# All down projections of the FFN stages in two rounds of 256 tokens, and the stages' activation tiles moved to 0 modulo 256 bytes

## The reference, cut to what matters

```python
def swiglu(u, w_gate_up, w_down):            # stage "f", D_FF = 2816
    gate, up = jnp.split(u @ w_gate_up, 2, axis=-1)
    return (jax.nn.silu(gate) * up) @ w_down

def sqrelu_mlp(x, w1, w2):                   # stages "m" and "n", D_FF_2 = 4096
    h = jax.nn.relu(x @ w1)
    return (h * h) @ w2
```

## Time and profile before

| | |
|---|---|
| median of 3 runs | 2082.5 us (2082.31 to 2082.69) |
| profiled execution, own time | 2082.63 us |
| its span | 2080.8 us |
| TensorE busy (matmul) | 2066.9 us, 99%, 12658 matmuls |
| VectorE, ScalarE, GpSimd busy | 1526.3, 982.3, 720.8 us |
| granted TensorE clock | full in all slices of the page |
| DMA | 188.44 MB, mean 91 GB/s |

### The profile page before, as it was taken

One profiled execution on the slowest core, in us unless ns is written; L12 is line 12 of the kernel. 1 busy time (PEld: TensorE's weight loads), 2 busy tenths in 40 slices (PEclk: granted clock), 3 DMA queues, 4 the chain that ended last, 5 costly groups with the idle time before them and its releaser, 6 DMA issues.

```text
span 2080.8 us, 32208 instructions
## 1 busy us (share of the span) xinstructions
PE 2066.9 (99%) x12658; PEld 1751.4 (84%) x12658; DVE 1526.3 (73%) x2087; ACT 982.3 (47%) x1656; POOL 720.8 (35%) x595
## 2 busy tenths in 40 slices
PE   9999999999999999999999999999999999999999
PEld 7888688888999998877789999988975678898988
DVE  6866775658988886388768787866578757877776
ACT  4433564445444444456554333344527755343433
POOL 2301520027443334064463232301147746333321
PEclk9999999999999999999999999999999999999999
DMA  6233135223333433211133323232530012333331
GB/s 182 91 107 86 52 102 172 71 66 95 102 103 102 121 93 101 81 51 52 41 92 104 120 82 122 83 120 89 152 80 1 2 52 75 118 93 110 93 110 51
DMA packets 293590, 188.44 MB, mean 91 GB/s; under 512 B 9280, under 2 KB 287040, under 8 KB 293440
## 3 DMA queue, kind: packets, MB, share of 16 engines
q1 hardware_dynamic: 293152, 186.18, 29.9%
q10 hardware_dynamic: 288, 0.21, 0.0%
HBM read 183.48 MB, written 2.10 MB: 89 GB/s over the span
## 4 chain that ended last, share of the span: by engine, by line
PE 94%; DVE 3%; ACT 1%; issue 1%; DMA 0%; POOL 0%; DVEq 0%; SPq 0%; ACTq 0%
PE ps L544 92%; PE ps L578 2%; DVE wl L517 1%; ACT wh L507 1%; DVE sb_small L3456 0%; DMA p_xt<-in_x 0%; DVE ns_x L3502 0%; DVE ns_x L3501 0%; DVE H L673 0%; DVE nt_pts L3484 0%; ACT XH L565 0%; ACT xb_x L565 0%; DVE tp_up L2296 0%; DVE tp_up L2309 0%; DVE XL L573 0%
## 5 line engine op out<-in xcount | busy, mean ns | idle before, releaser
L517 DVE TENSOR_TENSOR wl<-raw,wh 128x1024 fp32r<-128x1024 f32 (+1 forms) x334 | 429.4, 1300 | 231.9 <-ACT wh L507 231.3
L544 PE MATMUL ps<-xb_x,wh 128*128 128x256 f32 (+1 forms) x1584 | 388.8, 336 | 1.5 <-DVE st_k L2758 0.6
L507 ACT CAST wh<-raw 128x1024 fp32r<-128x1024 f32 (+1 forms) x334 | 322.0, 980 | 129.0 <-PE ps L544 119.4
L544 PEld LDWEIGHTS ps<-xb_x,wh 128*128 128x128 f32 x1584 | 267.2, 189 | 30.1 <-DVE H L673 0.9
L544 PE MATMUL ps<-tt_t,wh 128*128 128x256 f32 x1536 | 272.4, 279 | 0.9 <-ACT tp_q L2243 0.5
L544 PE MATMUL ps<-xb_x,wl 128*128 128x256 f32 (+1 forms) x792 | 265.0, 335 | 0.0
L544 PEld LDWEIGHTS ps<-tt_t,wh 128*128 128x128 f32 x1536 | 235.7, 188 | 4.8 <-ACT tp_q L2243 1.2
L544 PE MATMUL ps<-XH,wh 128*128 128x512 f32 (+1 forms) x616 | 227.2, 369 | 1.2 <-DVE H L703 0.8
L544 PE MATMUL ps<-XH,wl 128*128 128x512 f32 (+1 forms) x616 | 222.2, 361 | 0.0
L544 PE MATMUL ps<-XL,wh 128*128 128x512 f32 (+1 forms) x616 | 222.0, 360 | 0.0
L544 PE MATMUL ps<-tt_t,wl 128*128 128x256 f32 x768 | 213.1, 277 | 0.0
(11 more groups left out here) (448 smaller groups left out, 4566.9 us busy)
## 6 DMA issues: line engine op xcount, KB each, us to landing
raw<-in_mlp_w SPq DMA_DIRECT2D x128, 512.0 KB, 4.1
raw<-in_w_gate_up SPq DMA_DIRECT2D x44, 512.0 KB, 4.0
raw<-in_w_in SPq DMA_DIRECT2D x28, 512.0 KB, 3.7
raw<-in_sb_w_qkv SPq DMA_DIRECT2D x24, 512.0 KB, 3.6
raw<-in_w_down SPq DMA_DIRECT2D x22, 512.0 KB, 6.0
raw<-in_w_out_mix SPq DMA_DIRECT2D x16, 512.0 KB, 3.5
raw<-in_w_kv SPq DMA_DIRECT2D x16, 512.0 KB, 3.7
raw<-in_nsa_w_kv SPq DMA_DIRECT2D x12, 512.0 KB, 3.8
```

The source lines that it names most:

```text
L507: e.copy(shaped(WH[i % NH], i), source(i)).then_inc(*w_hi.up(i))
L517: e.tensor_tensor(shaped(WL[i % NH], i), source(i), shaped(WH[i % NH], i).bitcast(F), ALU.subtract).then_inc(*w_lo.up(i))
L544: return e.matmul(out, a, b, start=start, stop=stop, skip_group_check=True)
```

## The change

1. A new function `pe_down` replaces the call of `project` for downs. It runs over the tokens in two halves of 256 columns each, with all weight blocks in each half; the halves go to the two halves of the same PSUM bank. The matmuls double in number and halve in width. The release to VectorE stays one for the whole bank.
2. The plain activations of f and m move from xb (at PH0) to `XF` at PH0 - 64; those of n from XH and XL to `XN` at XAT + 192. The hidden tiles of f and m move from XAT to XAT + 192, those of n from PH0 to PH0 - 64. By the offsets in the code: XF and the hidden tiles of n start at 127232, XN and the hidden tiles of f and m at 77568; both are 0 modulo 256 (and 256 modulo 512). TT stays.
3. `sb_small` is placed ahead of rs, to make room for XN (which ends at 110336; rs then starts at 110400).

The last group of n keeps its own function, and reads the moved hidden tiles.

```diff
+    sb_small = sb("sb_small", [128, 64])
     RS0 = base[0]
...
-    sb_small = sb("sb_small", [128, 64])
     base[0] += 192
     PH0 = base[0]
     XB = Pair(*(Phase(PH0 + 4 * 8 * S * i, f"xb{i}").sb("x", [128, 8, S], R) for i in range(2)))
+    XF = Pair(*(Phase(PH0 - 64 + 4 * 8 * S * i, f"xf{i}").sb("x", [128, 8, S], R) for i in range(2)))
+    XN = Pair(*(Phase(XAT + 192 + 4 * 8 * S * i, f"xn{i}").sb("x", [128, 8, S], R) for i in range(2)))
...
-                act_hi(e, XB, "ff", o - 1, H[:, o - 1, :], col("ffn_norm", o - 1))
+                act_hi(e, XF, "ff", o - 1, H[:, o - 1, :], col("ffn_norm", o - 1))
...
                 if kind == "down":
                     t = take(e, key)
                     per = 8 // self.groups[g]
-                    project(e, self.units[n], self.hid[g % 2], f"{self.tag}{g}", t[:, :], key, nk=self.groups[g],
-                            c=128 * (c % per))
+                    self.pe_down(e, n, t, g, 128 * (c % per))
...
+        def pe_down(self, e, n, t, g, c):
+            i, hid = UI[self.units[n]], self.hid[g % 2]
+            e.wait_ge(*w_lo.at(i))
+            wh, wl = shaped(WH[i % NH], i), shaped(WL[i % NH], i)
+            last = self.groups[g] - 1
+            for half in range(2):
+                at = slice(256 * half, 256 * half + 256)
+                for k in range(last + 1):
+                    e.wait_ge(*x_lo.at(f"{self.tag}{g}", k))
+                    mm(e, t[:, at], wh[:, k, c:c + 128], hid.hi[:, k, at], k == 0, False)
+                    mm(e, t[:, at], wh[:, k, c:c + 128], hid.lo[:, k, at], False, False)
+                    f = mm(e, t[:, at], wl[:, k, c:c + 128], hid.hi[:, k, at], False, k == last)
+            f.then_inc(*proj.up(self.tag, n))
+            if not proj.final:
+                proj.name("unit", i)
...
-    ff = Ffn("f", GU, "ff", XB, XAT, "xa", [(v_made, ("xq", 7))])
-    fm = Ffn("m", [4] * 8, "m", XB, XAT, "st", [(g_made, ("fe", 7))])
-    fn = Ffn("n", [4] * 8, "n", X, PH0, "ns", [(v_made, ("nq", 7))], halves=True)
+    ff = Ffn("f", GU, "ff", XF, XAT + 192, "xa", [(v_made, ("xq", 7))])
+    fm = Ffn("m", [4] * 8, "m", XF, XAT + 192, "st", [(g_made, ("fe", 7))])
+    fn = Ffn("n", [4] * 8, "n", XN, PH0 - 64, "ns", [(v_made, ("nq", 7))], halves=True)
```

More of the change, by code:

```diff
@@ L1924, in act_xattn @@
         e.wait_ge(*h_new.at("xa", 7))
-        act_hi(e, XB, "ff", 7, H[:, 7, :], col("ffn_norm", 7))
+        act_hi(e, XF, "ff", 7, H[:, 7, :], col("ffn_norm", 7))
         act_square(e, "ff", 7, H[:, 7, :])
@@ L2005, in low @@
             e.wait_ge(*h_new.at("xa", o))
-            dve_lo(e, XB, "ff", o, H[:, o, :], col("ffn_norm", o))
+            dve_lo(e, XF, "ff", o, H[:, o, :], col("ffn_norm", o))
         for o in range(8):
@@ L2691, in act_stick @@
                 e.wait_ge(*h_new.at("st", o - 1))
-                act_hi(e, XB, "m", o - 1, H[:, o - 1, :], col("ng", 8 + o - 1))
+                act_hi(e, XF, "m", o - 1, H[:, o - 1, :], col("ng", 8 + o - 1))
                 act_square(e, "m", o - 1, H[:, o - 1, :])
@@ L2695, in act_stick @@
         e.wait_ge(*h_new.at("st", 7))
-        act_hi(e, XB, "m", 7, H[:, 7, :], col("ng", 15))
+        act_hi(e, XF, "m", 7, H[:, 7, :], col("ng", 15))
         act_square(e, "m", 7, H[:, 7, :])
@@ L2813, in low @@
             e.wait_ge(*h_new.at("st", o))
-            dve_lo(e, XB, "m", o, H[:, o, :], col("ng", 8 + o))
+            dve_lo(e, XF, "m", o, H[:, o, :], col("ng", 8 + o))
         for o in range(8):
@@ L3408, in act_nsa @@
                 e.wait_ge(*h_new.at("ns", o - 1))
-                act_hi(e, X, "n", o - 1, H[:, o - 1, :], col("ng", 24 + o - 1))
+                act_hi(e, XN, "n", o - 1, H[:, o - 1, :], col("ng", 24 + o - 1))
                 act_square(e, "n", o - 1, H[:, o - 1, :])
@@ L3412, in act_nsa @@
         e.wait_ge(*h_new.at("ns", 7))
-        act_hi(e, X, "n", 7, H[:, 7, :], col("ng", 31))
+        act_hi(e, XN, "n", 7, H[:, 7, :], col("ng", 31))
         act_square(e, "n", 7, H[:, 7, :])
@@ L3634, in low @@
             e.wait_ge(*h_new.at("ns", o))
-            dve_lo(e, X, "n", o, H[:, o, :], col("ng", 24 + o))
+            dve_lo(e, XN, "n", o, H[:, o, :], col("ng", 24 + o))
         for o in range(8):
```

## The result

| | before | after |
|---|---|---|
| median | 2082.7 us (2082.31 to 2082.98, 6 runs) | 2089.7 us (2087.67 to 2091.17, 6 runs) |
| ratio | | 1.0034 (1.0023 to 1.0045) |
| profiled execution, span | 2082.63, 2080.8 us | 2088.78, 2087.0 us |

The kernel is slower by 7 us, where 14 us less were forecast. The page of the kernel after, to set against the earlier trace rows: busy time by engine, the chain that ended last, and two groups of halved downs (count, busy us, mean ns).

A forecast was written before the change was run, and what follows sets the result against it. TensorE, busy 99%, was taken as the bound: matmul count times start-to-start distance. Pairs and downs -9.0 and -5.6, swallowed by waits +1.4, tail -1.3, nearer wait +0.5 gave -14.0: 2068.5 us from 2082.5; range 2064 to 2093.

The forecast's parts named there:

- the first rival: FFN stages: 256-column matmuls stay at 117.8 ns, 12.0 us more per stage; one slow stage 0.16, two or three 0.13.
- the quick cadence: FFN stages: aligned 256-column matmuls start 113.3 ns apart; holding in all three stages had chance 0.50, at 2068.5 us.
- Blocks of m: Stage m, one pair and four downs: 20.72 us becomes 20.40, 0.32 less in each of 14 blocks.
- Blocks of n: Stage n, one pair and four downs: 20.72 us becomes 20.40, 0.32 less in each of 14 blocks.
- Stage f: Gated stage, ten blocks of two pairs and four downs: 0.56 us less each, 5.6 in all, two blocks' gain swallowed.
- First jobs: Four plain 512-column jobs ahead of each stage's pairs, 288 matmuls: stay at 226.7 ns, taken as 0, at most 3.8 us less.
- the nearer x_lo wait: Last groups: half downs meet the fourth hidden tile's late low part; 0.2 us each in f and m, 0.1 in the tail.
- The tail: Its 192 half matmuls read the moved hidden tiles and go from 120.0 to 113.3 ns: 1.3 us less.
- The splitting: Downs in two halves: itself brings nothing, since 2 x 113.3 is 226.7 ns, what one whole down matmul takes.
- The rule of the Trainium skill: Matmul distance is N/2.4 + 2.5 ns, so splitting 1968 downs would add 4.9 us and the sum would be -9.
- The second rival: FFN tiles: 512-byte alignment is needed, so pairs stay at 120.0 ns and split downs cost 240.0; 2107 us, chance 0.08.

The follow-up runs named there:

- the rhythm held fast: Kernel after plus three extra same-remainder matmuls ahead of one pair each in n and m and f's first downs behind pairs, first jobs whole: 2074.4 us, ratio 0.9961.

## Why the prediction was wrong

**The step that failed** is the one by which the first rival was put at 0.29 in place of a half or more: "the quick cadence holds without a break, the stalls of the gated stage end in it". The rhythm does persist by itself; it does so in both forms. Behind the hiccups at four earlier downs f went on fast, behind the one at 627 us slow, and n was slow from its first pair. The forecast named what held it in check before (the plain products at 120.0) and that the change removes them, and then argued from rows in which they still stood. The earlier trace rows had shown that a wait can end either way; with nine waits in f, two of which left the slow rhythm, and nothing that resets, how f ended hung on the last of them. Why that one left the slow rhythm isn't shown; it did so again in the kernel with only the first jobs in halves. Of the stages the text said that their 512-column jobs "could put the first pair at 117.8 and nothing but a stall would take it out", which is what happened in n for the whole stage, and in f until its first stall at 510 us. In m the same jobs put the first pair at 113.3.

**Point by point.**

- Blocks of m: 20.40 us as forecast. The stage is 4.5 us shorter, for which 4.2 stood in the sum (14 x 0.32 less 0.3 for its first pairs).
- Blocks of n: 20.40 forecast, 21.20 measured; 6.3 us longer than before in place of 4.5 less. This is 10.8 of the 20 us between forecast and result.
- Stage f: from its first to its last combined product 1.7 longer in place of some 4.5 shorter, 6.2 of the 20 us; the last twelve downs behind it, slow as well, add 288 x 4.4 ns = 1.3.
- First jobs: taken at 0 with bounds from 0 to -3.8; measured +6.7 ns each, 288 x 6.7 = +1.9 us, and the three kernels with the weights moved show that it goes with the two remainders. I had bounded an operation that no row showed only from below ("From above, nothing"), and it came out above.
- Waits: the nearer x_lo wait is there before the last group of m (0.35 us for 0.2 forecast); in f it did not come. Not foreseen were the 0.1 us at the first down behind a pair in f. By themselves they cost nothing that counts; the one of them at 627 us cost the stage its rhythm.
- The tail, with its many waits, runs now in the one and now in the other rhythm; behind the last combined product it is 0.5 us shorter, where 1.3 less 0.1 for its wait were forecast.
- The splitting costs nothing when the rhythm is fast (30 halves in 3.40 us), as forecast. The rule of the Trainium skill ("TensorE: Matmul & The Clock Gate", Back-to-back issue gap), which the page gives as the gap of an isolated matmul and which was weighed in the prediction with its fixed part of 2.5 ns for each, doesn't describe either form: 256 columns took 113.3, 117.8 or 120.0 and 512 took 226.7 or 233.3, by addresses and history.
- The second rival (256 bytes isn't what counts) was put down to 512 and is refuted in that form: tiles at 256 modulo 512 ran at 113.3. In a form that I hadn't thought of it is true, since the weights' remainder is what counts.

In sum: 10.8 + 6.2 + 1.3 + 1.9 = 20.2 us, and 2068.5 + 20.2 = 2088.7 against the profiled execution's 2088.8; what m, the tail and the waits add and take away cancels to 0.1. With the rhythm held fast (2074.4) what is left over the forecast is 5.9 us, of which the 33 extra matmuls are 3.8 and the first jobs 1.9.

**What stays open.** Theory and runs agree on the persistence, but for the one turn without a wait with the weights at 192. What in the engine holds the two rhythms, and why two extra matmuls turn it over while three bring the fast one: the runs show the behaviour, not its cause. Why the same 512-column jobs leave m in the fast rhythm and n in the slow one isn't shown either. That executions of one kernel differ because its stages come in either rhythm fits the numbers of the two kernels that spread by 10 us and more, but only one execution of each has a trace. In the same way the rhythms of every kernel here are read from one execution; for the two with three extra matmuls and whole first jobs the other times agree with them (2073.97 to 2075.37, and 2093.67 to 2094.46 but for the 2104.69).

## What to carry to other kernels

Before a tile is moved, write down both operands' start addresses modulo 256: for 256 columns in float32r another remainder than the weights' was up to 6.7 ns a matmul quicker here, for 512 columns up to 6.7 ns slower. Where a slow-looking step is removed from a stream of matmuls, ask what state it had been resetting, and test the stream over a whole stage, not over one product. An operation that no row shows is bounded from above as well.

## What the runs showed of the hardware

Distance from start to start at the full granted clock, float32r, by the weights' (stationary) start less the moving operand's, modulo 256 bytes; ns, with the pairs of remainders (moving/stationary) seen:

| less | 256 columns | 512 columns | seen at |
|---|---|---|---|
| 0 | 120.0 | 226.7 | 64/64, 0/0; for 512 also 128/128, 192/192 |
| 64 | 113.3 or 117.8, lasting | 233.3 | 0/64; for 512 also 64/128, with 229 in some stretches |
| 128 | 118.7 (115 to 122 by turns) | 231.6 to 233.3 | 0/128; for 512 also 64/192 |
| 192 | 113.3 or 117.8, lasting | 228.8 to 230.3 | 0/192; for 512 also 64/0, with 233 in some stretches |

The 512-column figures are means of twelve in a row. The rhythm lasts over 280 us and some 2400 matmuls without a wait (stage n of the kernel after) and passes from one product, bank and tile to the next. It turned behind waits that made one distance 148 ns (537 us in f) or 193 ns (627 us), behind three matmuls of some 120 ns each (567 us in f, with three extra), and once, with the weights at 192, behind nothing that the trace shows.
